# Feed-forward products in rows, 512 wide, with transposed hidden tiles, in a transformer kernel on one core

## The chip, the core and the metric

One core of a Trainium2 chip runs the whole program. Its engines work side by side and hand over by semaphores: TensorE (PE in the profile; PEld is its load of the stationary operand), VectorE (DVE), ScalarE (ACT), GpSimd (POOL) and SyncE (SP, which issues the loads here). Each engine carries out its own instructions in the order in which they are written. SBUF is the working memory of 128 partitions, PSUM (`ps`, 8 banks of 128 x 512 float32) takes TensorE's results. The metric is the device time of one execution in microseconds (us); lower is better.

## The reference

256 tokens of width 1024, float32, go through two blocks, one stage after the other. Each stage is `x = x + rms_norm(f(rms_norm(x, g_pre)), g_post)`, in the second block's feed-forward stages with a factor of 0.5 on the added part. The nine stages are:

```
moba    spatial gating, block attention of 8 heads and a causal convolution, then w_out
cross   attention to 256 rows of memory, 4 heads of 256
relu    square(relu(h @ w_ff1)) @ w_ff2, hidden width 4096
glu0    (silu(h @ wg) * (h @ wu)) @ wd, hidden width 2816
diff    differential attention, 8 heads of 2 x 64, rotary
glu1    as glu0
glu2    as glu0 (second layer)
near    neighborhood attention, 16 heads of 64
glu3    as glu0
```

`rms_norm(x, g)` is `x * rsqrt(mean(x * x) + 1e-6) * g` by token.

## The kernel before

**Products.** Float32 accuracy comes from splitting each operand into a high part of type float32r and the rest (low part), and adding three products: high x high, low x high, high x low. Weights come in chunks of 1 MB (`CH` = 2048 columns of 128 partitions): SP loads a chunk into one of three `raw` slots, ScalarE casts it to `w_hi` (L504, in loops L513), VectorE subtracts to `w_lo` (L756, in loops L765), TensorE uses it and signals `used`. 226 chunks are used, in one fixed order. Chunk c + 3 is split when chunk c has been used.

**Two forms of product.** `transposed_product` (L1146 to L1148) keeps a 128 x 128 block of weights in the array and streams the 256 tokens of `hT`: 48 matmuls of 256 columns a chunk; the result has features in partitions. `rows_product` (L1160 to L1162) keeps 128 tokens in the array and streams weights: the result has tokens in partitions. Down and output products are such, 24 matmuls of 512 columns a chunk, into the four banks `ps[2t + nb]` for token half t and column half nb. Values (`v`, `w`, `V`) are rows too, 256 columns wide.

**Feed-forward stages.** They run in loops (`Fori`) over blocks of 256 hidden columns: a gate chunk (bank 4), an up chunk (bank 5) and a down chunk; relu has only up and down. ScalarE applies Silu or Relu (`gate`), VectorE multiplies (`hraw`), and as the result already has features in partitions, it is cast and split to `hid_hi` and `hid_lo` (L683, L1053) and is the stationary operand of the down product.

**Attention stages.** `PLAN` writes out the order of the words for every engine: `q0` is a chunk, `rot0` a rotary step, a number an attention step, `o0` an output chunk. In step s the scores of unit s are computed, the probabilities of unit s - 1 are transposed (L1207) and the values of unit s - 2 weighed; in diff the result of unit s - 3 is transposed too. Products of chunks stand between the steps and fill TensorE while VectorE and ScalarE work on the softmax.

**The norm between two stages.** For token half t: ScalarE squares the two banks of y and sums (L541), POOL takes the root (L445, L446), VectorE multiplies y by the gain (L805) and adds it to x (L815), then multiplies x by the next gain into `t1` (L780). ScalarE squares x (L524), POOL takes the next root, VectorE writes it on a diagonal (L789), and TensorE multiplies `t1` by the diagonal in 8 matmuls, which transposes and scales at once (`turn`, L1175). ScalarE casts the two banks to `hT_hi` (L531), VectorE subtracts to `hT_lo` (L795). VectorE's order is written out: scale_y(0), add_y(0), gain_rows(0), scale_y(1), diagonal(0), add_y(1), gain_rows(1), low part 0, diagonal(1), low parts 1 to 3, and after them two splits of chunks. ScalarE: four squares of y, four of x, four casts, one split. The next stage's first product waits for `h_lo` of both halves.

## Time and profile before

| | |
|---|---|
| three runs, us | 1544.32, 1548.31, 1548.76 (median 1548.31) |
| profiled execution, us | 1547.44, of which span of the trace 1545.7 |
| mean granted TensorE clock | 0.981 |
| instructions | 24401 |
| PE busy | 1462.8 us, 95% |
| DVE busy | 856.8 us, 55% |
| ACT busy | 681.0 us, 44% |
| POOL busy | 141.8 us, 9% |
| loads | 255.95 MB, mean 166 GB/s |

Busy time is what an engine spends in instructions; a busy PE is not one at its peak, since matmuls overlap, so the distance between the starts of two matmuls says more than the duration of one. The granted clock is the share of 2.4 GHz that TensorE was given; it has two levels, 1.2 and 2.4 GHz. The time of an execution is the span and some 1.7 us around it.

### The profile page before, as it was taken

What the parts mean: (1) busy time and instruction counts of PE and PEld (TensorE: products, weight loads), DVE (VectorE), ACT (ScalarE), POOL (GpSimd) and SP (SyncE); (2) the same over time, 40 slices, a digit from 0 to 9 for tenths busy, and PEclk for the clock granted to TensorE, in tenths of its full rate; (3) what the DMA queues carried; (4) which work ended last, traced back from release to release, by engine and by line L of the source; (5) the groups of instructions that cost most, each with busy time, mean ns of one, the idle gap of its engine ahead of it and who ended that gap; (6) DMA issues with size and microseconds to landing.
All of it is one profiled execution on the core that took longest, in us unless ns stands there. A gap on an engine that the chain in (4) does not pass through costs nothing.

```text
span 1545.7 us, 24401 instructions
## 1 busy us (share of the span) xinstructions
PE 1462.8 (95%) x9945; PEld 1341.6 (87%) x9945; DVE 856.8 (55%) x912; ACT 681.0 (44%) x878; POOL 141.8 (9%) x248
## 2 busy tenths in 40 slices
PE   6999898999989999898889999899998999899996
PEld 6997687999989999897779999899997887799996
DVE  4976546555565454567655444655445656554443
ACT  5455444444453334445444433434434544444432
POOL 1000101111010110100111110111102300100000
PEclk9999999999999999999999999999999999999998
DMA  9654243565645566342336556465654534265551
GB/s 291 197 187 137 86 160 114 192 195 194 213 128 190 193 196 217 123 153 91 128 111 196 194 181 214 131 198 194 195 189 141 164 109 137 63 210 190 183 179 59
DMA packets 186889, 255.95 MB, mean 166 GB/s; under 512 B 6280, under 2 KB 163660, under 8 KB 186828
## 3 DMA queue, kind: packets, MB, share of 16 engines
q1 hardware_dynamic: 182732, 251.94, 50.0%
q0 software_dynamic: 4096, 3.15, 0.7%
q8 instruction: 43, 0.70, 0.2%
q14 instruction: 18, 0.15, 0.0%
HBM read 254.02 MB, written 1.05 MB: 165 GB/s over the span
## 4 chain that ended last, share of the span: by engine, by line
PE 89%; DVE 3%; ACT 3%; POOL 2%; issue 1%; DMA 1%; SPq 0%; DVEq 0%; POOLq 0%; ACTq 0%
PE ps L1146 17%; PE ps L1147 17%; PE ps L1148 17%; PE ps L1160 11%; PE ps L1161 10%; PE ps L1162 10%; PE ps L1175 2%; PE ps L1235 2%; PE ps L1196 2%; PE ps L1207 1%; DVE w_lo L756 1%; POOL rstd L445 1%; POOL rstd L446 1%; ACT t L565 1%; DMA raw<-w_in 1%
## 5 line engine op out<-in xcount | busy, mean ns | idle before, releaser
L1146 PE MATMUL ps<-hT_hi,w_hi 128*128 128x256 f32 x2096 | 597.7, 285 | 6.2 <-DVE hT_lo L795 4.8
L1147 PE MATMUL ps<-hT_lo,w_hi 128*128 128x256 f32 x2096 | 593.5, 283 | 0.0
L1148 PE MATMUL ps<-hT_hi,w_lo 128*128 128x256 f32 x2096 | 593.4, 283 | 0.0
L765 DVE TENSOR_TENSOR w_lo<-raw,w_hi 128x2048 fp32r<-128x2048 f32 x132 | 302.6, 2292 | 231.4 <-ACT w_hi L513 231.4
L1146 PEld LDWEIGHTS ps<-hT_hi,w_hi 128*128 128x128 f32 x2096 | 402.6, 192 | 12.5 <-issue 8.5
L1147 PEld LDWEIGHTS ps<-hT_lo,w_hi 128*128 128x128 f32 x2096 | 402.6, 192 | 2.6 <-issue 0.5
L1148 PEld LDWEIGHTS ps<-hT_hi,w_lo 128*128 128x128 f32 x2096 | 402.5, 192 | 0.0
L513 ACT CAST w_hi<-raw 128x2048 fp32r<-128x2048 f32 x132 | 250.9, 1901 | 118.6 <-PE ps L1148 118.6
L756 DVE TENSOR_TENSOR w_lo<-raw,w_hi 128x2048 fp32r<-128x2048 f32 x94 | 215.8, 2303 | 83.8 <-ACT w_hi L504 83.5
L504 ACT CAST w_hi<-raw 128x2048 fp32r<-128x2048 f32 x94 | 179.0, 1904 | 52.3 <-PE ps L1148 24.0
L1160 PE MATMUL ps<-w_hi,hid_hi 128*128 128x512 f32 x440 | 171.9, 391 | 0.0
L1161 PE MATMUL ps<-w_lo,hid_hi 128*128 128x512 f32 x440 | 171.8, 391 | 0.0
L1162 PE MATMUL ps<-w_hi,hid_lo 128*128 128x512 f32 x440 | 171.2, 389 | 0.0
L433 POOL DMA_DIRECT2D big<-na_rpb x128 | 66.1, 517 | 565.4 <-PE ps L1148 384.6
L683 ACT CAST hid_hi<-t 128x512 fp32r<-128x512 f32 x55 | 34.1, 620 | 174.2 <-PE ps L1162 174.2
L1175 PE MATMUL ps<-rope_t,t 128*128 128x128 f32 x320 | 58.9, 361 | 46.4 <-DVE rope_t L789 46.4
L1175 PEld LDWEIGHTS ps<-rope_t,t 128*128 128x128 f32 x320 | 55.2, 269 | 51.4 <-issue 51.4
L1162 PEld LDWEIGHTS ps<-w_hi,hid_lo 128*128 128x128 f32 x440 | 82.6, 188 | 17.6
L1160 PEld LDWEIGHTS ps<-w_hi,hid_hi 128*128 128x128 f32 x440 | 82.8, 188 | 15.7
L1161 PEld LDWEIGHTS ps<-w_lo,hid_hi 128*128 128x128 f32 x440 | 82.8, 188 | 15.1
L1160 PE MATMUL ps<-w_hi,yT_hi 128*128 128x512 f32 (+1 forms) x232 | 86.0, 371 | 3.1 <-DVE yT_lo L1014 3.0
L1053 DVE TENSOR_TENSOR hid_lo<-t,hid_hi 128x512 fp32r<-128x512 f32 x55 | 38.1, 692 | 90.6 <-ACT hid_hi L683 90.6
(162 smaller groups left out, 1506.9 us busy)
## 6 DMA issues: line engine op xcount, KB each, us to landing
raw<-ffn_wg SPq DMA_DIRECT2D x44, 1024.0 KB, 5.6
raw<-ffn_wu SPq DMA_DIRECT2D x44, 1024.0 KB, 5.6
raw<-ffn_wd SPq DMA_DIRECT2D x44, 1024.0 KB, 5.2
raw<-w_ff SPq DMA_DIRECT2D x32, 1024.0 KB, 5.4
raw<-diff_w_in SPq DMA_DIRECT2D x12, 1024.0 KB, 5.1
raw<-na_w_in SPq DMA_DIRECT2D x12, 1024.0 KB, 5.1
raw<-w_in SPq DMA_DIRECT2D x10, 1024.0 KB, 5.7
raw<-w_xkv SPq DMA_DIRECT2D x8, 1024.0 KB, 5.5
```

The source lines that it names most:

```text
L433: pool.dma_start(bias[p:p + 1], bass.AP(rpb.tensor, (5 - r) * 31 + 15 - c, [[465, 16], [31, 6], [1, 64]])).then_inc(bias_in, 16)
L504: act.copy(w_hi[:, slot, :], raw[:, slot, :]).then_inc(hi_done, 1)
L513: act.copy(w_hi[:, slot, :], raw[:, slot, :]).then_inc(hi_done, 1)
L756: dve.tensor_tensor(w_lo[:, slot, :], raw[:, slot, :], w_hi[:, slot, :], ALU.subtract).then_inc(lo_done, 1)
L765: dve.tensor_tensor(w_lo[:, slot, :], raw[:, slot, :], w_hi[:, slot, :], ALU.subtract).then_inc(lo_done, 1)
L1146: pe.matmul(o, hi, src[0][:, k, :], start=(k == 0), stop=False)
L1147: pe.matmul(o, hi, src[1][:, k, :], start=False, stop=False)
L1148: ins = pe.matmul(o, lo, src[0][:, k, :], start=False, stop=(k == KT - 1))
L1160: pe.matmul(o, hi, wh[:, i, cols], start=first and i == 0, stop=False)
L1161: pe.matmul(o, hi, wl[:, i, cols], start=False, stop=False)
L1162: ins = pe.matmul(o, lo, wh[:, i, cols], start=False, stop=last and i == len(tiles) - 1)
L1175: ins = pe.matmul(ps[:, 4 + 2 * t + b, k * P:(k + 1) * P], t1[:, t, col:col + P], diag[:, t, :], start=True, stop=True)
```

## The change

The feed-forward stages no longer use the transposed form for gate and up. They are now rows products over blocks of 512 hidden columns: chunk `ga` holds the first four tiles of 128 input features by 512 columns, `gb` the other four, and both add into one bank a token half (`up`). ScalarE's Silu or Relu and VectorE's multiplication give `hraw` with tokens in partitions; TensorE transposes it back in 128 x 128 blocks (`hidden_turn`, word `T`) into the bank of the up product, and the cast and the low part go from there to `yT`, which is the stationary operand of the down product. The last block of a gated stage is 256 wide (`g`, `u`, `d`). The values of diff and near are computed so too, ahead of q and k (`va` to `vd`), into banks 4 to 7.

Where the next stage is a feed-forward stage (`LATE_SCALE`), the pre-norm's root isn't put on a diagonal: `turn` is a plain transpose, and `rstd` is the scale of Silu or Relu and of the multiplication (in relu it enters twice, in a gated stage once in each factor).

There are four slots for split weights in these stages; the fourth lies over `qT` and `kT` (`w_hi_3`, `w_lo_3`). `raw` keeps three. All loops are gone: the whole program is a list of words in `PLAN`, which all engines read. `s` is a split of the next chunk on ScalarE and VectorE, `h` on ScalarE alone, `l` on VectorE alone; `q1.0` and `q1.1` are the halves of a product. `G` and `H` are activation and multiplication of a block, `T` its transposing with cast and low part.

The norm is five words for each token half: `post` (squares of y, root, scale, add), `gain`, `sq` (squares of x, root, and the diagonal where there is one), `turn` (transposing, casts, low parts), with 0 at the end of a stage and 1 at the head of the next. Each engine carries out its part of each word in the order of the words. The gains are loaded at the seventh and eighth chunk of a stage.

Core of the diff:

```diff
+HEAD_GLU = "post1 s gain1 s turn1 sq1 ga0 s gb0 G0.0 G0.1 s ua0 s ub0 H0.0 H0.1 s "
+BLOCK_GLU = ("ga{b} s T{a} gb{b} G{b}.0 G{b}.1 s ua{b} s ub{b} H{b}.0 H{b}.1 s da{a} s db{a} s ")
+LAST_GLU = ("g5 T4 G5.0 G5.1 s u5 H5.0 H5.1 s da4 T5 ")
+GLU = HEAD_GLU + "".join(BLOCK_GLU.format(a=b - 1, b=b) for b in range(1, 5)) + LAST_GLU
+HEAD_RELU = ("post1 s gain1 s turn1 sq1 ua0 s ub0 G0.0 H0.0 G0.1 H0.1 s ua1 s T0 "
+             "ub1 G1.0 H1.0 G1.1 H1.1 s da0 s db0 s ")
+BLOCK_RELU = "ua{b} s T{a} ub{b} G{b}.0 H{b}.0 G{b}.1 H{b}.1 s da{a} s db{a} s "
+RELU = (HEAD_RELU + "".join(BLOCK_RELU.format(a=b - 1, b=b) for b in range(2, 7)) +
+        "ua7 s T6 ub7 G7.0 H7.0 G7.1 H7.1 s da6 T7 s db6 s da7 db7 ")
+HEAD_V = "post1 s gain1 sq1 s turn1 va0 s vb0 s vc0 "
+PLAN = {
...
+    "relu": RELU + "post0 gain0 turn0 sq0",
+    "glu0": GLU + "s db4 d5 post0 gain0 sq0 turn0",
...
+    "diff": (HEAD_V + "s vd0 "
+             "q0 s k0 s rot0 q1.0 rot4 q1.1 h lambda 0 l k1.0 rot1 k1.1 h 1 l q2.0 rot5 q2.1 h 2 l "
+             "k2.0 rot2 k2.1 h 3 l q3.0 rot6 q3.1 h 4 l k3.0 rot3 k3.1 h 5 l rot7 o0.0 6 o0.1 h 7 l "
+             "o1.0 8 o1.1 s 9 s o2 10 o3 post0 gain0 turn0 sq0"),
+    "glu1": GLU + "s db4 d5 post0 gain0 turn0 sq0",
+    "glu2": GLU + "s db4 d5 post0 gain0 sq0 turn0",
+    "near": (HEAD_V + "vd0 s "
...
+             "q0 s k0 s 0 q1.0 1 q1.1 h 2 l k1.0 3 k1.1 h 4 l q2.0 5 q2.1 h 6 l k2.0 7 k2.1 h 8 l "
...
+    "glu3": GLU + "db4 d5 post0 end1",
...
+LATE_SCALE = {i + 1 for i, kind in enumerate(STAGES) if kind in FFN}
...
+    held, slots, before = [-1] * 4, [], []
+    for c, (kind, name, _) in enumerate(CHUNKS):
+        free = range(4) if kind in FFN or name in ("va", "vb", "vc", "vd") else range(3)
+        slot = min(free, key=lambda s: held[s])
+        slots.append(slot)
+        before.append(held[slot])
+        held[slot] = c
...
+        w_hi_3 = nc.alloc_sbuf_tensor_at("w_hi_3", [P, CH], F32R, offset=qk_end - 16 * KT * P)
+        w_lo_3 = nc.alloc_sbuf_tensor_at("w_lo_3", [P, CH], F32R, offset=qk_end - 8 * KT * P)
...
-        hraw = t1[:, 0, 0:512]
-        gate = t1[:, 0, 512:1024]
...
+        def turn_bank(n, t, b):
+            return ps[:, 5 + 2 * b if n >= 2 else 4 + 2 * t + b, :]
+        def up_bank(kind, b, t):
+            return ps[:, (4 + 2 * (b % 2) if kind == "relu" else 6) + t, :]
...
+                if c == FIRST[at] + 6:
+                    load_post_gain(at)
+                load(c, src, dims)
+                if c == FIRST[at] + 7 and at < N_NORMS - 1:
+                    load_pre_gain(2 + at)
...
+            def norm_word(word):
+                t, j, n = norm_at(word)
+                if word.name in ("post", "end"):
                     for b in range(2):
+                        if b == 0:
+                            act.wait_ge(y_bank, 2 * j + t + 1)
                         else:
+                            act.wait_ge((half_used, used)[t], LAST[j] + 1)
+                        count = 2 * (TT * j + t) + b + 1
+                        square(ps[:, 2 * t + b, :], b, ssq[:, 32 + TT * j + t, b:b + 1], sq_post, count)
+                if word.name == "sq":
+                    for b in range(2):
+                        act.wait_ge(x_new, 2 * (TT * j + t) + b + 1)
+                        count = 2 * (TT * n + t) + b + 1
+                        square(x[:, t, 512 * b:512 * b + 512], b, ssq[:, TT * n + t, b:b + 1], sq_pre, count)
...
+                    src = up_bank(kind, b, t) if kind == "relu" else ps[:, 4 + t, :]
+                    act.activation(gate[:, t, 0:width], src[:, 0:width], ACT.Relu if kind == "relu" else ACT.Silu,
+                                   scale=rstd[:, k:k + 1]).then_inc(gate_done, 1)
...
+            def norm_word(word):
+                t, j, n = norm_at(word)
+                if word.name in ("post", "end"):
+                    scale_y(j, t)
+                    add_y(j, t)
+                if word.name == "gain":
+                    gain_rows(n, x, t)
+                if word.name == "sq" and n not in LATE_SCALE:
+                    diagonal(n, t)
+                if word.name == "turn":
+                    turned_lo(n, t, hT)
...
+            def hidden_word(kind, word):
+                b, t, beta = word.digit, word.half, B0[kind] + word.digit
+                if word.name == "H":
+                    last = "b" if kind == "relu" or b < 5 else ""
+                    width = 256 if kind != "relu" and b == 5 else 512
+                    dve.wait_ge((half_used, used)[t], AT_CHUNK[kind, "u" + last, b] + 1)
+                    dve.wait_ge(gate_done, TT * beta + t + 1)
+                    if b:
+                        dve.wait_ge(hid_turned, TT * (beta - 1) + t + 1)
+                    k = TT * (word.at + 1) + t
+                    dve.scalar_tensor_tensor(hraw[:, t, 0:width], up_bank(kind, b, t)[:, 0:width], rstd[:, k:k + 1],
+                                             gate[:, t, 0:width], ALU.mult, ALU.mult).then_inc(hraw_done, 1)
...
+            def turn(n, t):
+                if n >= 2 and t:
+                    pe.wait_ge(h_lo, 4 * n + 2)
+                late = n in LATE_SCALE
+                if not late:
+                    pe.wait_ge(diag_set, len([m for m in range(n) if m not in LATE_SCALE]) * TT + t + 1)
+                for b in range(2):
+                    pe.wait_ge(normed, 2 * (TT * n + t) + b + 1)
+                    for k in range(4):
+                        rows, to = t1[:, t, P * (4 * b + k):P * (4 * b + k) + P], turn_bank(n, t, b)[:, k * P:(k + 1) * P]
+                        if late:
+                            ins = pe.transpose(to, rows, ident)
+                        else:
+                            ins = pe.matmul(to, rows, diag[:, t, :], start=True, stop=True)
+                    ins.then_inc(turned, 1)
...
+            def hidden_turn(kind, word):
+                b, beta = word.digit, B0[kind] + word.digit
+                for t in range(TT):
+                    pe.wait_ge(hraw_done, TT * beta + t + 1)
+                    for i in range(len(hid_tiles(kind, b))):
+                        cols = slice(i * P, i * P + P)
+                        ins = pe.transpose(up_bank(kind, b, t)[:, cols], hraw[:, t, cols], ident)
+                    ins.then_inc(hid_turned, 1)
...
+            def up(kind, word):
+                b, beta = word.digit, B0[kind] + word.digit
+                short = len(word.name) == 1
+                first, last = word.name[1:] in ("a", ""), word.name[1:] in ("b", "")
+                tiles = range(KT) if short else range(4 * last, 4 * last + 4)
+                width = 256 if short else 512
+                for t in halves_of(word):
+                    for i in range(2) if short else (int(last),):
+                        h_ready(word.at + 1, t, i)
+                    if first and kind == "relu" and b >= 2:
+                        pe.wait_ge(hid_lo, TT * (beta - 2) + t + 1)
+                    if first and kind != "relu" and b >= 1:
+                        if word.name[0] == "g":
+                            pe.wait_ge(gate_done, TT * (beta - 1) + t + 1)
+                        else:
+                            pe.wait_ge(hid_lo, TT * (beta - 1) + t + 1)
+                    o = ps[:, 4 + t, :] if word.name[0] == "g" else up_bank(kind, b, t)
+                    finish(in_rows(hT, tiles, word, width, o[:, 0:width], t, 0, first, last), word, t)
...
+            def values(kind, word):
+                i = "abcd".index(word.name[1])
+                for t in halves_of(word):
+                    h_ready(word.at + 1, t, i % 2)
+                    o = ps[:, 4 + 2 * (i // 2) + t, :]
+                    tiles = range(4 * (i % 2), 4 * (i % 2) + 4)
+                    finish(in_rows(hT, tiles, word, 512, o, t, 0, i % 2 == 0, i % 2 == 1), word, t)
```

In `turn`, n >= 2 and t = 1 waits for the low parts of half 0, since both halves now use banks 5 and 7. Words in which an engine has no part are skipped by it; TensorE has none in `post`, `gain` and `sq`.

## Rows read from the trace of the kernel before

**Rows 1.** The page, busy us (share of the span) x instructions.

```profile
PE 1462.8 (95%) x9945; PEld 1341.6 (87%) x9945; DVE 856.8 (55%) x912; ACT 681.0 (44%) x878; POOL 141.8 (9%) x248
```

**Rows 2.** Busy us by stretch, last product of a stage to next product.

```profile
core 0: us, PE busy (x) PEld busy (x) DVE busy (x) ACT busy (x) POOL busy (x), PEclk, DMA share, GB/s
439.10:450.36 11.26, 6.73 (x33) 6.19 (x33) 8.14 (x14) 5.61 (x15) 3.46 (x6) 0.70 0.00 0
...
1184.06:1196.07 12.01, 6.39 (x33) 5.94 (x33) 8.87 (x14) 4.94 (x13) 8.18 (x11) 0.72 0.00 0
...
175.17:185.62 10.45, 5.70 (x33) 5.24 (x33) 8.15 (x14) 5.61 (x15) 3.46 (x6) 0.84 0.00 0
...
sum 88.53, PE 50.04 PEld 46.15 DVE 66.19 ACT 42.77 POOL 32.42; mean PE 6.25 PEld 5.77 DVE 8.27 ACT 5.35 POOL 4.05
```

**Rows 3.** The same view: relu, glu0, diff and near, first to last product.

```profile
257.54:439.10 181.56, 180.11 (x1152) 164.05 (x1152) 97.97 (x69) 79.04 (x71) 17.48 (x34) 1.00 0.60 195
450.36:637.19 186.83, 186.83 (x1320) 176.12 (x1320) 93.30 (x60) 77.12 (x63) 17.34 (x34) 1.00 0.60 195
648.40:788.28 139.88, 125.53 (x880) 114.10 (x880) 88.07 (x139) 66.50 (x149) 10.44 (x18) 0.98 0.39 128
1196.07:1334.68 138.61, 136.92 (x866) 112.42 (x864) 80.95 (x141) 67.30 (x124) 17.77 (x14) 1.00 0.40 130
```

**Rows 4.** Timeline, PE: start us, us, line, op, out<-in, shape; two product forms.

```profile
245.04 0.39 PE L1160 MATMUL ps<-w_hi,yT_hi 128*128 128x512 f32 x1
...
246.18 0.39 PE L1162 MATMUL ps<-w_hi,yT_lo 128*128 128x512 f32 x1
...
460.02 0.28 PE L1148 MATMUL ps<-hT_hi,w_lo 128*128 128x256 f32 x1
...
460.74 0.28 PE L1148 MATMUL ps<-hT_hi,w_lo 128*128 128x256 f32 x1
```

**Rows 5.** Timeline, PE: four transposes of probabilities and the next product.

```profile
120.18 0.66 PE L1207 MATMUL ps<-tab,prob 128*128 128x128 f32 x4
120.59 0.36 PE L1146 MATMUL ps<-hT_hi,w_hi 128*128 128x256 f32 x1
```

**Rows 6.** Timeline, relu to glu0: ACT, DVE and POOL; in brackets idle before.

```profile
437.37 0.30 POOL L445 TENSOR_SCALAR rstd<-ssq 128x1 f32<-128x1 f32 x1 [25.50 <-ACT probT L541]
...
438.34 1.42 DVE L815 SCALAR_TENSOR_TENSOR x_rows<-t,rstd,x_rows 128x512 f32<-128x512 f32 x2 [0.35 <-POOL rstd L446]
...
439.30 0.60 ACT L541 ACTIVATE prob<-ps 128x512 f32<-128x512 f32 x1 [0.67 <-PE ps L1162]
...
439.68 1.28 DVE L780 TENSOR_TENSOR t<-x_rows,gain 128x512 f32<-128x512 f32 x2
...
448.91 0.59 ACT L531 CAST hT_hi<-ps 128x512 fp32r<-128x512 f32 x1 [1.34 <-PE ps L1175]
...
450.28 1.92 ACT L504 CAST w_hi<-raw 128x2048 fp32r<-128x2048 f32 x1
...
450.42 0.69 DVE L795 TENSOR_TENSOR hT_lo<-ps,hT_hi 128x512 fp32r<-128x512 f32 x1 [0.20 <-ACT hT_hi L531]
451.03 2.28 DVE L756 TENSOR_TENSOR w_lo<-raw,w_hi 128x2048 fp32r<-128x2048 f32 x1
```

**Rows 7.** Timeline, PE: the last product of relu.

```profile
438.87 0.39 PE L1162 MATMUL ps<-w_hi,yT_lo 128*128 128x512 f32 x1
```

**Rows 8.** Busy us by stretch, columns as in rows 2: the low clock.

```profile
443.19:448.63 5.44, 5.44 (x24) 5.19 (x25) 3.96 (x7) 2.56 (x6) 1.08 (x2) 0.50 0.00 0
...
178.98:182.39 3.41, 3.12 (x15) 3.15 (x15) 3.09 (x6) 1.97 (x5) 1.01 (x2) 0.50 0.00 0
```

**Rows 9.** Timeline, DVE: two low parts in diff, one step in near.

```profile
733.55 0.42 DVE L1014 TENSOR_TENSOR yT_lo<-ps,yT_hi 128x256 fp32r<-128x256 f32 x1
...
744.58 0.42 DVE L1014 TENSOR_TENSOR yT_lo<-ps,yT_hi 128x256 fp32r<-128x256 f32 x1
...
1244.29 0.76 DVE L954 SCALAR_TENSOR_TENSOR att_bias<-ps,big 128x256 f32<-128x256 f32 x2 [1.66 <-PE ps L1196]
```

**Rows 10.** Timeline, PE: weighing the values in one step of diff.

```profile
734.12 1.13 PE L1222 MATMUL ps<-vv,probT 128*128 128x128 f32 x8 [1.42 <-DVE yT_lo L1014]
```

904 lines of the change are left out of this document (386 added, 518 removed), and 14 rows, old and new, of the table PLAN.

## The prediction

> **What bounds the kernel now.** I read the busy table first: TensorE is busy for 95% of the span [rows 1], so only what changes its own work or its pauses can matter. Then the table by stretches [rows 2, 3], cut at every point where TensorE starts no product for over 10 us. Eight such stretches, the norms between two stages, sum to 88.53 us [rows 2]. They are 10.45 us (moba to cross; cross to relu the same), 12.01 us (glu2 to near) and between 10.5 and 11.3 us for the rest. Between them TensorE is full: in glu0 186.83 us busy of 186.83 [rows 3], in relu 180.11 of 181.56, in near 136.92 of 138.61. Only diff has real pauses, 14 of 139.88 us. Third, the distance of matmul starts: 256-wide products start every 0.12 us (460.02 to 460.74, six steps), 512-wide ones every 0.228 us (245.04 to 246.18, five steps) [rows 4]. A chunk of weights is 48 narrow or 24 wide matmuls, 5.76 or 5.46 us; glu0's 22 up and gate chunks and 11 down chunks give 22 x 5.76 + 11 x 5.46 = 186.8, the measured length. So the model of products is right, and the loops of that stage cost nothing that can be seen. Last, the timeline of one norm, relu to glu0 [rows 6, 7]. I call E the end of the last product there: last start 438.87 + 0.23 = 439.10. The next product starts 11.26 us later [rows 2].
>
> **Wide products.** These narrow chunks become wide: 16 in relu, 20 of 22 in each gated stage (the last gate and up chunk stay 256 wide), 4 values chunks each in diff and near. Each saves 5.76 - 5.46 = 0.30 us: relu -4.8, each gated stage -6.0, diff and near -1.2 each; together -31.2.
>
> **The transposes this buys.** A hidden block of 512 in rows needs 8 transposes before the down product: 8 blocks in relu, five of 8 and one of 4 in each gated stage, 240 in all. The same operation stands in the attention steps: four transposes start at 120.18 and the next product follows at 120.59 [rows 5]. That is 0.41 us for four, plus about 0.1 for leaving a product: 1.0 for eight, 0.6 for four. Relu +8.0, each gated stage +5.6, together +30.4. Bounds: 0.82 us a group of eight (nothing lost at the ends) to 1.2. The Trainium skill (TensorE: Matmul & The Clock Gate, Part 4: PE-mode transpose) gives about 275 ns for one such transpose in a kernel; 240 of them would then be 66 us and the total 40 us higher. The row of this case has starts 0.11 us apart and decides.
>
> Does TensorE wait for these hidden tiles? A T word is written one to three chunks behind the product that makes its rows, 5.5 us or more, while activation and multiply take 0.6 + 0.7. After T, ScalarE first casts a chunk (1.92), then two tiles (0.59 each), VectorE splits (2.28), then takes the low parts (0.69): about 5.0 us to the first half [rows 6]. The next user (ua after gb) comes 1.0 + 5.46 = 6.5 us after T began, so 1.5 us are spare. The exception is T4 then u5 in the gated stages: u5 writes the bank that T4 fills. First four transposes 0.7, cast 0.6, low part 0.7 and hand-overs: 2.1 against 1.0 of TensorE work, a stall of 1.1 us, four times: +4.4.
>
> Against measured stages: a gated stage becomes 31 x 5.46 + 2 x 5.76 + 5.6 + 1.1 = 187.5 for 186.83 (+0.6, four times +2.4); relu 32 x 5.46 + 8.0 = 182.7 for 181.56 (+1.2; that stage also loses a wait of its own). **Feed-forward stages: +3.6.**
>
> **The row scale.** Moving the scale from the diagonal to gate and up costs nothing: same instructions with a scalar operand. It takes the root and the diagonal off the chain of the norm. **Four weight slots, no loops.** Splits ran one chunk ahead already without TensorE waiting; nothing is gained, and nothing lost, since hand-written stretches like near run as densely as looped ones [rows 3]. **Queue of SP.** The gains are loaded at the stage's seventh and eighth chunk; their waits (y_scaled and normed of the norm before) are long met, and 0.5 MB beside chunks that come three buffers ahead is hidden. **Queue of POOL.** The roots stand in the order of the words and the 128 loads of na_rpb keep their counts of used chunks, none ahead of a root that a product waits for: nothing.
>
> **The norm between stages.** This decides. In after, both VectorE and ScalarE execute it word by word: post0 gain0 turn0 sq0 | post1 s gain1 s turn1 sq1. Token half 1 can start only when half 0 has gone through TensorE and back, and two chunk splits stand inside it; TensorE stands at turn1, which is written before ga0. With durations of [rows 6, 7], in us after E: add of half 0 ends 0.66 and its gain 1.86 (both as before); turn0's second four transposes give their bank at 2.7; two casts 3.3; ScalarE then squares x (a pair, 2 x 0.6 + 0.1 = 1.3) to 4.6, and only then y of half 1, whose bank was ready at 0.2, to 6.0; POOL's root with its hand-overs (437.37 to the add's start at 438.34), 7.0; add 1.42, 8.45; the split s 2.28, 10.75 (its ScalarE cast is over at 7.9); gain 1.28, 12.05; turn1's last four transposes at half clock, twice the 0.41, 12.95. There ga0's half 0 starts: it needs nothing of half 1, whose low parts come (behind the second split) at 15.0, before its 12 matmuls are over. So 12.95 instead of 11.3 (or 10.5) us. Five stages begin so: cross to relu, relu to glu0, diff to glu1, glu1 to glu2, near to glu3.
>
> The three into attention (sq0 before turn0) keep the diagonal: x squared 1.5, root 2.5, diagonal 2.85, turn0 4.2, casts 4.9, y squared 6.2, root 7.2, add 8.6, split 10.9, gain 12.2, diagonal 12.5, eight slow turns 14.5. diff and near start va0 there: 14.5. cross starts with q0, which needs both halves: cast 0.59 and low parts 0.69 more, 15.95. Sum: 5 x 12.95 + 2 x 14.5 + 15.95 = 109.7 against 88.53: **+21.2**. Bounds: if each hand-over is 0.1 us shorter or POOL's root 0.6 us longer, as it is elsewhere, -8 to +8.
>
> **The clock.** Before, it is at its lower level (1.2 GHz) for a part of each norm: the granted share over a norm is 0.70 to 0.84 [rows 2]. TensorE takes up work inside the low part and has 3.12 us (178.98 to 182.39) or 5.44 us (443.19 to 448.63) of it behind it when the clock is back [rows 8]. The 16 turns absorb that, so products start at 2.4 GHz. After, TensorE does 1 us of turn0, pauses until E + 11.45, and products follow the few transposes at once. With 4.3 us to come back the clock rises at E + 15.8: 2.8 us of products at half speed, 1.4 lost, five times 7.0; diff and near 1.2 each, cross 0.5. **+10**, bounds 0 (risen by the transposes) and 18 (the longer return everywhere).
>
> **diff and near.** The values chunks go ahead of the attention steps, which are then filled by halves of q, k and output chunks. near: two half-chunk steps take 11.4 us of TensorE; VectorE has 1.66 us idle in such a pair already [rows 9], so it stays TensorE's: -1.2 + 0.6 for the first step's chain = -0.6. diff: six steps carry a rope and a split; VectorE needs 11.0 us for one (low part at 733.55 to low part at 744.58) and holds TensorE up by 1.42 us [rows 9, 10]. Those keep their length; the steps with half chunks and no rope come down to 7 to 9 us from 8 to 10 us; the front gets 40.4 instead of 31.5 us. Sum 139 for 139.88: -1, with -6 and +5 as bounds, for I had to lay these steps in a row from single durations. moba and cross keep their order.
>
> **Sum.** +3.6 + 21.2 + 10 - 1 - 0.6 = +33.2 on the profiled execution's 1547.44 us (span 1545.7): 1580.6. The median of the three runs is 0.9 us higher. I take 1581.
>
> **Rivals.**
> (a) The norm is set by the data alone, not by the written order: the squares of y of half 1 follow its bank, and the splits fall elsewhere. Then E + 0.2, squares 1.5, root 2.5, add 3.9, gain 5.2, turn 5.6: 5.6 us for late-scale stages, 7.5 for diff and near, 9 for cross, 52 in all instead of 88.5, hardly any slow clock: -36.5 + 3.6 - 1.6, about **1513**. For it: the chain with no root and diagonal is really shorter, and half 0 alone opens the stage. Against it: each engine takes its queue in order, and VectorE is in between for at least one split. It decides if half 1's add ends before E + 5 rather than at 8.5.
> (b) The gaps stay as they are (the shorter chain and the splits just cancel) and the clock is up in time: only +3.6 - 1.6: **1549**, no change.
> (c) Hidden tiles come late in every block, as the spare 1.5 us is used up by cast or split order: 1 us each in 30 blocks, **1611**. Against: those engines are half idle in glu0 (93 and 77 of 187 us).
> (d) Turns of late-scale stages leave the clock low for their 1.4 us too, half of it lost five times: 3.5 more, **1584**. The Trainium skill (the same section) says that transposes don't count as busy for the clock; no row here has them alone with a low clock, while the turns of [rows 8] are true matmuls.
>
> **Chances.** Forecast 0.66 (own range 1560 to 1600: norms, clock and diff near their ends), (d) 0.05, (c) 0.09, (b) 0.06, (a) 0.14. The range leaves out (a) and the far end of (c): 1546 to 1611. About 0.3%, 4.6 us, is what a measurement of this kernel tells from none. Faster than that 0.14, within 0.06, slower 0.80.
>
> **What would show it.** Right: stretches without product of 13 to 16 us, with squares of y (t=1) some 4.7 us after E, a split between the second add and the second gain; slow clock over the first matmuls of a stage; glu0 187 to 190 us from first to last product; transposes 0.11 us apart. Wrong: stretches under 10 us, waits of ua on hidden tiles, or values chunks in diff leaving the steps idle by over 15 us more.

## The result, and the profile of the changed kernel

The changed kernel takes 1614.03 us (median of 4 runs, 1613.15 to 1616.0); the kernel before took 1547.92 us in 4 runs beside it (1544.32 to 1548.76). The ratio is 1.0434, with a 95% interval from 1.0414 to 1.0453. So it is slower, as forecast, but by 66 us and not by 33, and just outside the range.

The profiled execution took 1616.0 us, its span is 1614.3 us, the mean granted clock 0.955 for 0.981. From the page, the busy line (as rows 1):

```profile
PE 1460.8 (90%) x7609; PEld 1236.1 (77%) x7609; DVE 852.2 (53%) x910; ACT 688.8 (43%) x886; POOL 142.0 (9%) x248
```

TensorE has 2336 instructions fewer and is busy for 2 us less, but its share fell from 95% to 90%: the added time is pauses, and products at the low clock.

The stretches from the last product of a stage to the next product, columns as in rows 2:

```profile
180.00:200.12 20.12, 7.24 (x33) 6.54 (x33) 11.20 (x16) 8.08 (x17) 4.81 (x6) 0.67 0.22 79
...
458.89:471.51 12.62, 3.01 (x17) 2.46 (x17) 10.39 (x13) 7.62 (x13) 1.72 (x4) 0.68 0.08 16
659.10:677.87 18.77, 7.35 (x34) 6.93 (x33) 12.72 (x16) 9.29 (x17) 4.82 (x6) 0.56 0.23 79
...
1238.84:1258.12 19.28, 7.14 (x33) 6.82 (x33) 14.06 (x16) 9.28 (x17) 9.37 (x9) 0.66 0.25 82
...
sum 121.30, PE 36.77 PEld 32.59 DVE 90.00 ACT 64.74 POOL 27.62; mean PE 4.09 PEld 3.62 DVE 10.00 ACT 7.19 POOL 3.07
```

These are moba to cross, relu to glu0, glu0 to diff, glu2 to near. The five norms ahead of a feed-forward stage are alike (12.61 to 12.65 us). All eight sum to 121.3 for 88.53 us [rows 2]: **+32.8**. (The means in the last row count a ninth stretch, of 0.01 us.)

The same view of the stages relu, glu0, diff and near, first to last product:

```profile
275.91:458.89 182.98, 182.98 (x834) 151.80 (x832) 94.14 (x69) 78.59 (x72) 18.39 (x36) 0.99 0.59 193
471.51:659.10 187.59, 186.53 (x886) 156.44 (x884) 90.26 (x62) 76.40 (x66) 18.25 (x36) 0.99 0.59 194
677.87:837.96 160.09, 131.04 (x786) 113.73 (x785) 84.20 (x137) 63.41 (x145) 10.44 (x18) 0.90 0.32 103
...
1258.12:1401.62 143.50, 137.30 (x770) 108.67 (x769) 75.61 (x140) 63.15 (x120) 17.98 (x16) 0.99 0.34 114
```

Against rows 3: relu +1.4, glu0 +0.8, **diff +20.2**, near +4.9. In diff TensorE pauses for 29.1 us where it paused for 14.4 (+14.7), and is busy for 131.04 us for 125.53 (+5.5) at a mean clock of 0.90 for 0.98. The other stages, from the same starts and ends of products: moba +4.8 (0.4 of it ahead of its first product), cross +1.7, all five feed-forward stages together +4.1. Nothing is added behind the last product. This is 68.6 us, by which the two profiled executions differ too.

Where the low clock falls differs from kernel to kernel, and this moves stages that an edit doesn't touch. cross takes 61.46 us (within 0.01) in the kernel before and in every run that has no low clock in it, and 63.18 here, where 3.9 us of it are at the low clock:

```profile
200.12:263.30 63.18, 62.50 (x368) 56.41 (x368) 26.98 (x35) 24.54 (x39) 0.86 (x2) 0.97 0.37 125
```

moba, ahead of every norm, takes 161.1 us with 3.4 us at the low clock in this kernel, and 163.4 with 10.2 in those of experiments 5 and 7. So a difference of one to three us between two kernels is put down to an edit below only where a row shows it.

### The profile page after: what moved, and what is told of

Same layout as the page of the kernel before. It is cut to its first block, busy times and chain, and to the rows that moved or that the text cites. A ratio compares the mean times of both kernels' runs of the same rounds, so it can differ in the third digit from the quotient of the medians.

```text
span 1614.3 us, 18455 instructions
## 1 busy us (share of the span) xinstructions
PE 1460.8 (90%) x7609; PEld 1236.1 (77%) x7609; DVE 852.2 (53%) x910; ACT 688.8 (43%) x886; POOL 142.0 (9%) x248
## 3 DMA queue, kind: packets, MB, share of 16 engines
HBM read 254.02 MB, written 1.05 MB: 158 GB/s over the span
## 4 chain that ended last, share of the span: by engine, by line
PE 85%; DVE 5%; ACT 4%; issue 3%; POOL 2%; DMA 1%; SPq 0%; DVEq 0%; ACTq 0%; POOLq 0%
PE ps L1107 22%; PE ps L1109 22%; PE ps L1108 22%; PE ps L1093 4%; PE ps L1094 3%; PE ps L1095 3%; PE ps L1184 2%; PE ps L1145 2%; PE ps L1126 2%; PE ps L1333 2%; DVE w_lo L771 1%; ACT probT L560 1%; PE ps L1156 1%; DVE x_rows L820 1%; POOL rstd L487 1%
## 5 line engine op out<-in xcount | busy, mean ns | idle before, releaser
L1107 PE MATMUL ps<-w_hi,hT_hi 128*128 128x512 f32 (+1 forms) x1008 | 380.3, 377 | 4.2 <-DVE yT_lo L1060 4.2
L1108 PE MATMUL ps<-w_lo,hT_hi 128*128 128x512 f32 (+1 forms) x1008 | 375.6, 373 | 0.0
L1109 PE MATMUL ps<-w_hi,hT_lo 128*128 128x512 f32 (+1 forms) x1008 | 375.5, 373 | 0.0
L1107 PE MATMUL ps<-w_hi,yT_hi 128*128 128x512 f32 (+1 forms) x672 | 260.2, 387 | 13.3 <-DVE rope_t L1035 7.5
L1109 PE MATMUL ps<-w_hi,yT_lo 128*128 128x512 f32 (+1 forms) x672 | 257.1, 383 | 0.0
L1107 PEld LDWEIGHTS ps<-w_hi,hT_hi 128*128 128x128 f32 x1008 | 192.0, 190 | 37.4 <-issue 5.5
L1109 PEld LDWEIGHTS ps<-w_hi,hT_lo 128*128 128x128 f32 x1008 | 191.3, 190 | 33.5
L1107 PEld LDWEIGHTS ps<-w_hi,yT_hi 128*128 128x128 f32 x672 | 127.8, 190 | 42.4 <-DVE w_lo L771 12.1
L1093 PE MATMUL ps<-hT_hi,w_hi 128*128 128x256 f32 x432 | 128.5, 298 | 3.2 <-DVE hT_lo L800 3.2
L1094 PE MATMUL ps<-hT_lo,w_hi 128*128 128x256 f32 x432 | 123.7, 286 | 0.0
L1095 PE MATMUL ps<-hT_hi,w_lo 128*128 128x256 f32 x432 | 123.4, 286 | 0.0
L1093 PEld LDWEIGHTS ps<-hT_hi,w_hi 128*128 128x128 f32 x432 | 84.4, 195 | 9.3 <-issue 8.9
L1094 PEld LDWEIGHTS ps<-hT_lo,w_hi 128*128 128x128 f32 x432 | 84.4, 195 | 0.8 <-issue 0.5
L1095 PEld LDWEIGHTS ps<-hT_hi,w_lo 128*128 128x128 f32 x432 | 84.3, 195 | 0.0
```

What stands on the lines that cost most here:

```text
L1093: pe.matmul(o, hi, src[0][:, k, tokens], start=(k == 0), stop=False)
L1094: pe.matmul(o, hi, src[1][:, k, tokens], start=False, stop=False)
L1095: ins = pe.matmul(o, lo, src[0][:, k, tokens], start=False, stop=(k == KT - 1))
L1107: pe.matmul(o, hi, wh[:, i, cols], start=first and i == 0, stop=False)
L1108: pe.matmul(o, hi, wl[:, i, cols], start=False, stop=False)
L1109: ins = pe.matmul(o, lo, wh[:, i, cols], start=False, stop=last and i == len(tiles) - 1)
```

## Where each part of the time comes from

**A norm ahead of a feed-forward stage.** Timeline of relu to glu0 (start, duration, engine, line, operation; in brackets idle before), as rows 6; E, the last product's end, is 458.89:

```profile
465.56 1.41 DVE L820 SCALAR_TENSOR_TENSOR x_rows<-t,rstd,x_rows 128x512 f32<-128x512 f32 x2 [0.33 <-POOL rstd L487]
466.89 2.28 DVE L771 TENSOR_TENSOR w_lo<-raw,w_hi 128x2048 fp32r<-128x2048 f32 x1
469.09 1.28 DVE L785 TENSOR_TENSOR t<-x_rows,gain 128x512 f32<-128x512 f32 x2
469.92 1.94 PE L1124 MATMUL ps<-tab,t 128*128 128x128 f32 x8 [8.45 <-DVE t L785]
...
471.51 0.78 PE L1107 MATMUL ps<-w_hi,hT_hi 128*128 128x512 f32 x1
```

This is the forecast order: squares of y after squares of x, the add, a split between add and gain, the turn, the product at E + 12.62. TensorE idles for 8.45 us until half 1's gain is there.

**A norm ahead of attention.** Same view, glu0 to diff, E = 659.10:

```profile
662.15 3.79 PE L1126 MATMUL ps<-rope_t,t 128*128 128x128 f32 x16 [2.89 <-DVE rope_t L794]
...
670.13 2.29 DVE L771 TENSOR_TENSOR w_lo<-raw,w_hi 128x2048 fp32r<-128x2048 f32 x1
...
671.07 2.03 POOL L486 TENSOR_SCALAR rstd<-ssq 128x1 f32<-128x1 f32 x1 [2.31 <-ACT probT L560]
...
673.19 0.85 POOL L487 TENSOR_TENSOR rstd<-rstd,minus_half 128x1 f32<-128x1 f32 x1
674.08 0.29 DVE L794 TENSOR_SCALAR rope_t<-tab,rstd 128x128 f32<-128x128 f32 x1 [0.45 <-POOL rstd L487]
...
674.46 3.75 PE L1126 MATMUL ps<-rope_t,t 128*128 128x128 f32 x16 [8.53 <-DVE rope_t L794]
```

The eight matmuls with the diagonal are recorded as **x16**, two instructions ("passes" below) each: a turn is 3.8 us at the low clock, while the eight plain transposes of the fence above take 1.9, at the low clock too. I had priced both kinds by the count of instructions. And the root of half 1 waits on POOL: its two instructions take 2.03 and 0.85 us beside VectorE's split of a chunk, for 0.30 [rows 6] and some 0.56 us elsewhere. The first takes 2.03 us in all three norms ahead of attention, where it runs beside a split, and 0.52 in the same place of experiment 1, where the split is gone and only a gain runs beside it:

```profile
665.36 0.52 POOL L486 TENSOR_SCALAR rstd<-ssq 128x1 f32<-128x1 f32 x1 [2.30 <-ACT probT L560]
```

**diff.** TensorE waited over the whole kernel (us in total, times, longest), the first row of these for the norm's diagonals:

```profile
PE ps L1126 <- DVE rope_t L794: 45.7, 7, 10.8
PE ps L1107 <- DVE rope_t L1035: 7.5, 1, 7.5
PE ps L1145 <- issue: 5.8, 1, 5.8
...
PE ps L1107 <- DVE yT_lo L1060: 4.2, 4, 1.1
```

The places behind the third and the second of these rows, in TensorE's and VectorE's timeline:

```profile
738.40 2.29 DVE L771 TENSOR_TENSOR w_lo<-raw,w_hi 128x2048 fp32r<-128x2048 f32 x1
...
741.92 0.69 DVE L1039 TENSOR_TENSOR kT<-kT,rope_t 128x512 f32<-128x512 f32 x1
742.72 2.08 PE L1145 MATMUL ps<-kT,qT 64*128 64x256 f32 x8 [5.83 <-issue]
...
789.53 2.28 DVE L771 TENSOR_TENSOR w_lo<-raw,w_hi 128x2048 fp32r<-128x2048 f32 x1
791.73 0.68 DVE L1035 TENSOR_TENSOR rope_t<-ps,tab 128x512 f32<-128x512 f32 x1
...
792.66 0.77 PE L1107 MATMUL ps<-w_hi,yT_hi 128*128 128x512 f32 x1 [7.47 <-DVE rope_t L1035]
```

The first pause is put down to "issue", but the scores at 742.72 need `kT`, which VectorE ends at 742.6: the rotary step stands in the plan half a chunk before the attention step that uses it, and VectorE does a chunk's split first. A pause of 2.6 us ahead of 767.8 is the same. The third, 7.5 us, is the first output product, which waits for `rope_mul` 8 because it writes the banks of the last rotary step, again behind a split. In diff, waits for rotary steps are thus 17.4 us (7.5, 5.8 and two of 4.1 together), where the kernel before had 1.7. Of the others, the one for `yT_lo` fell from 9.4 to 5.4 us and the one for `sub_out` rose from 1.6 to 5.2.

**The end of moba.** The plan now splits a chunk ahead of the last attention step. In moba:

```profile
168.14 1.90 ACT L554 CAST w_hi<-raw 128x2048 fp32r<-128x2048 f32 x1 [3.42 <-PE ps L1109]
...
170.07 2.29 DVE L771 TENSOR_TENSOR w_lo<-raw,w_hi 128x2048 fp32r<-128x2048 f32 x1 [4.78 <-ACT w_hi L554]
172.28 0.42 DVE L1009 TENSOR_TENSOR yT_lo<-ps,yT_hi 128x256 fp32r<-128x256 f32 x1
...
172.84 0.47 PE L1107 MATMUL ps<-w_hi,yT_hi 128*128 128x512 f32 x1 [3.79 <-DVE yT_lo L1009]
```

Both halves of the split stand ahead of the two small operations that the last output product needs, and TensorE waits for 3.8 us, where it waited for 1.0 before. In near the same wait is 1.0 us, as before.

**near.** TensorE's waits between its first and last product:

```profile
PE ps L1145 <- ACT kT L698: 2.8, 4, 0.8
PE ps L1156 <- DVE prob L974: 2.4, 1, 2.4
```

The kernel before had the first once (0.7 us) and the second not at all. The 2.4 us are in the second attention step: the transposes of the first probabilities wait for the softmax, and only half a chunk stands in between.

## Experiments

Each kernel is the changed kernel with the edit shown, unless it says otherwise. Times are medians of 4 runs, the ratio is to the kernel before on the same chip (medians 1547.49, 1548.44, 1548.22 and 1549.78 us). The changed kernel is named C: 1614.03 us.

### 1. Chunk splits behind the norm

```diff
-HEAD_GLU = "post1 s gain1 s turn1 sq1 ga0
+HEAD_GLU = "post1 gain1 turn1 sq1 s s ga0
-HEAD_V = "post1 s gain1 sq1 s turn1 va0
+HEAD_V = "post1 gain1 sq1 turn1 s s va0
```

relu and cross are altered likewise.

> The changed kernel with the chunk splits of each stage's head moved behind turn1 (before they stood between post1 and gain1, and between gain1 and turn1). Theory W (the written order of the words sets the norm): in every norm one split of 2.3 us on VectorE leaves the chain, so the stretch without product falls from 12.6 to 10.3 us before a feed-forward stage and from 18.8 to 20.1 to some 16 to 17 us before an attention stage: 8 x 2.3 = 18 us less, 1596 us; a little more if POOL's root, slowed to 2.9 us beside a split, runs in 0.9. Rival C (the low clock is what costs, the split only fills a wait that another step sets): the stretches keep their length within 0.5 us, 1612 us.

Measured: 1603.77 us (ratio 1.036, 1.0342 to 1.0377), between the two expectations. Each feed-forward norm is 10.41 us for 12.62, so the split inside the norm costs 2.2 us, as its duration says; the attention norms lose 1.8 to 2.9. All norms together are 17.6 us shorter in the profile, but the stages are 4.3 us longer: glu3 takes 188.66 for 187.32 us,

```profile
1399.74:1588.40 188.66, 187.60 (x886) 157.20 (x884) 89.27 (x61) 76.78 (x68) 1.72 (x4) 0.99 0.47 159
```

with 4.4 us of its products at the low clock for 1.5. With the norm shorter, more of the low stretch lies on products. Of the 4.3 us, 2.6 are in feed-forward stages and 1.1 in near, which this explains; 1.1 are in moba, ahead of all norms. About a fifth of the gain is given back so.

### 2. Chunk splits behind the last attention step

```diff
-             "o1.0 8 o1.1 s 9 o2 post0 gain0 sq0 turn0"),
+             "o1.0 8 o1.1 9 s o2 post0 gain0 sq0 turn0"),
```

cross, diff and near likewise.

> The changed kernel with the splits that stand before the last attention steps of moba, cross, diff and near moved behind those steps (s 9 becomes 9 s, and the like). Theory W: the cast and the low part of the last heads wait behind a split of 1.9 + 2.3 us on ScalarE and VectorE, which is why moba ends 4.8 us later than before the change, near 4.9 and cross 1.7; moba gets 3.2 to 4.8 us back, near, cross and diff together 3 to 5: 1605 to 1608 us. Rival C (the half-speed clock after other pauses accounts for these stages): under 2 us, 1612 to 1614 us.

Measured: 1610.98 us (1.0402, 1.0385 to 1.042), 3 us of the 6 to 9 expected. moba fell from 161.11 to 158.13 us, and its wait of 3.8 us to 1.0; the rest over its length before, 1.5 us, goes with 3.4 us at the low clock. near stayed at 143.56 and diff at 159.98: there the place of this split was not the cause. cross fell from 63.18 to 61.46 us, its length before, but it does so in experiment 3 too, where its splits stand as in C; both runs have no low clock in it:

```profile
200.71:262.17 61.46, 60.78 (x368) 54.67 (x368) 26.96 (x35) 24.50 (x39) 0.86 (x2) 1.00 0.38 129
```

So the split did not lengthen cross; the low clock did.

### 3. Rotary steps one step earlier in diff

```diff
-"q0 s k0 s rot0 q1.0 rot4 q1.1 h lambda 0 l k1.0 rot1 k1.1 h 1 l q2.0 rot5 q2.1 h 2 l "
+"q0 s k0 s rot0 q1.0 rot4 q1.1 h lambda 0 rot1 l k1.0 k1.1 h 1 rot5 l q2.0 q2.1 h 2 rot2 l "
```

The other rotary steps move likewise, and the wait for `rope_mul` 8 goes from the first output product to where its second token half starts.

> The changed kernel with diff's rotary words moved to stand directly behind an attention step and ahead of the split that follows it, and with the first output product waiting for the rotary multiplications (banks 2 and 3) only at its second token half, which is the half that writes these banks. Theory R (three pauses of TensorE in diff, 5.8, 2.6 and 7.5 us, come from ropes that are written just ahead of their user): all 7.5 us and some 5 of the other 8.4 go, and part comes back as pauses elsewhere: diff from 160.1 to 145 to 150 us, kernel 1599 to 1604 us. Rival V (diff is bound by the softmax chain on VectorE and ScalarE, now that its values product stands ahead of it): diff stays above 155 us, kernel 1609 to 1614 us.

Measured: 1604.09 us (1.0366, 1.0349 to 1.0384), at the upper end of what was expected. diff, first to last product:

```profile
674.46:823.29 148.83, 128.68 (x786) 111.86 (x785) 83.75 (x137) 63.39 (x145) 10.45 (x18) 0.95 0.33 111
```

11.3 of the 20.2 us are gone: 8.9 of pauses and 2.4 of busy time; the clock of the stage is 0.95 for 0.90. The wait of 7.5 us is gone, the other waits for rotary steps are 6.9 us for 9.9 (one of 3.6 and three of 3.3 together), and the one for `yT_lo` is back from 5.4 to 7.0. TensorE still pauses for 20 us here where it paused for 14, and is busy for 3.2 us more than before; these two make the 9 us that are left.

### 4. Half 1 not behind half 0

```diff
-HEAD_GLU = "post1 s gain1 s turn1 sq1 ga0
+HEAD_GLU = "ga0
+LATE = "post0 gain0 post1 turn0 sq0 s gain1 s turn1 sq1"
+FULL = "post0 gain0 sq0 post1 turn0 s gain1 sq1 s turn1"
```

The plans end with LATE or FULL in place of `post0 gain0 ... turn0`, so ScalarE squares y of half 1 before it casts half 0.

> The changed kernel with all words of a norm at the end of the stage and post1 ahead of turn0, so that ScalarE and VectorE treat y of token half 1 without waiting for half 0's way through TensorE; the two splits keep their places around gain1. Theory W: before a feed-forward stage 12.6 becomes 10.1 us, before an attention stage 3 to 4 us less: 20 to 23 us less in all, 1591 to 1594 us. Rival C: as TensorE pauses as long, the clock falls as before and the first matmuls keep half speed, so that the gain is the same 20 us only if the return of the clock follows TensorE's work; if it comes at fixed times the gain is 10 to 15 us, 1599 to 1604 us.

Measured: 1601.68 us (1.0337, 1.0319 to 1.0354), above the first expectation and inside the rival's. Feed-forward norms 10.87 to 10.90 us, attention norms 18.05, 15.29 and 17.37, all eight together 16.2 us less. The stages are 3.7 us longer, but 2.1 of that are in moba, ahead of all norms, with 10.0 us at the low clock there for 3.4; feed-forward stages are 1.6 longer and near 1.0. So neither the written order nor the splits alone make the norm long, each is worth about as much, and each is partly given back by the clock.

### 5. The turn's waits filled with transposes

```diff
+                if n >= 2 and (t or not late):
+                    for _ in range(70 if t else 20):
+                        pe.transpose(ps[:, 4, 0:P], ident, ident)
```

> The changed kernel with 70 transposes of the identity, whose result nobody reads, written ahead of every turn1, and 20 ahead of each turn0 that waits for a diagonal. At full clock they take 0.11 us each, 7.7 and 2.2 us, which fits into TensorE's waits of 8.5 and 2.9 us. Theory K (the low clock costs beside the waits): if transposes hold the clock, the turns into attention run 32 passes at 0.11 instead of 0.21 us, 3.4 us less three times, and the first matmuls of all stages run at full speed, 1.0 to 1.6 us less eight times: 1614 - 20 = 1594 us. Rival N (transposes do not hold the clock): the 70 run at 0.21 us, 14.9 us, and lengthen each norm by 4 to 6 us: 1650 to 1660 us. Rival W (the clock costs nothing, only waits do): 1612 to 1616 us.

### 6. The same with matmuls

```diff
+                    for _ in range(35 if t else 10):
+                        pe.matmul(ps[:, 4, 0:P], ident, ident, start=True, stop=True)
```

> As the run with transposes, but with 35 and 10 float32 matmuls of the identity instead (two passes of 0.11 us each, so the same TensorE time). Theory K: they hold the clock, 1594 us as with transposes. If only these and not the transposes hold it, this run gives 1594 and the other 1650 us or more. Rival W: 1612 to 1616 us.

Measured: 1602.43 us with transposes (1.0349, 1.0328 to 1.0371) and 1606.87 with matmuls (1.0371, 1.0346 to 1.0396), whose intervals overlap. Both are 8 us or more above the 1594 of the theory and below the 1612 of rival W. Of the run with transposes, relu to glu0, glu0, and glu0 to diff by stretch, and TensorE's timeline in the two norms:

```profile
456.97:469.43 12.46, 9.91 (x88) 9.33 (x87) 10.25 (x13) 7.30 (x13) 1.72 (x4) 1.00 0.09 15
469.43:656.00 186.57, 185.51 (x887) 155.82 (x886) 90.37 (x62) 76.42 (x66) 18.17 (x36) 1.00 0.59 195
656.00:671.90 15.90, 13.80 (x123) 13.37 (x122) 12.03 (x15) 9.29 (x17) 4.82 (x6) 1.00 0.20 66
```

```profile
460.94 7.86 PE L1119 MATMUL ps<-tab 128*128 128x128 f32 x70 [1.40 <-DVE hT_lo L800]
...
659.05 2.05 PE L1129 MATMUL ps<-rope_t,t 128*128 128x128 f32 x16 [0.70 <-DVE rope_t L794]
```

In these two norms 70 transposes that compute nothing hold the clock at 2.4 GHz, as 35 two-pass matmuls do, and the turn of 16 passes takes 2.05 us where it took 3.79. Five of the eight norms are so. In the other three (cross to relu, diff to glu1, near to glu3) the clock fell in the pause ahead of the 70, and came back while TensorE did nothing but these transposes. Cross to relu, from the first of the 70 to the return of the clock, and from there to the last:

```profile
265.58:268.51 2.93, 2.93 (x14) 2.93 (x15) 1.54 (x3) 2.93 (x7) 1.72 (x4) 0.50 0.00 0
268.51:274.69 6.18, 6.18 (x59) 6.18 (x58) 6.18 (x6) 2.27 (x2) 0.00 (x0) 1.00 0.26 68
```

In the whole trace 54.5 us are at the low clock for 145.9 in C. Rival (d) of the prediction is gone with that. The Trainium skill (TensorE: Matmul & The Clock Gate, Part 4: PE-mode transpose) says that full clock doesn't engage for transposes; by this trace it is held through 7.86 us of nothing else and comes back with nothing else, and the measurement decides.

The kernel is 11.6 us faster by the medians and 13.3 by the profiled executions, but the low clock's price is larger. These became shorter: feed-forward stages 5.7, diff 3.5, near 1.5, cross 1.7, the three attention norms 8.6, together 21.0. Others became longer. The five norms ahead of feed-forward stages took 5.1 more, as the filling itself was on the path where the clock had fallen: from diff to glu1 its 70 took 10.80 us for 7.86, and the norm 15.42 for 12.65. moba and the time ahead of its first product took 2.6 more, with 10.2 us at the low clock for 3.4. So the 11.6 us are what the filling was worth, and not what the clock cost.

### 7. Every hidden tile transposed twice

```diff
-                    for i in range(len(hid_tiles(kind, b))):
+                    for i in 2 * tuple(range(len(hid_tiles(kind, b)))):
```

> The changed kernel with every hidden tile transposed twice into the same place. Theory T (the 240 transposes lie wholly on TensorE's path, 0.11 us each, and what they cost is what the wide products save): 26 us more, 1640 us; 1 to 2 more where u5 waits for T4. Rival H (they lie beside waits of TensorE and are partly hidden): under 15 us more.

Measured: 1635.92 us (1.0565, 1.0544 to 1.0586), +21.9 on C for 26 expected. relu by stretch:

```profile
276.04:465.73 189.69, 189.69 (x898) 158.61 (x896) 94.20 (x69) 78.52 (x72) 18.33 (x36) 0.99 0.57 186
```

relu grew by 6.7 us for 64 more transposes, the five feed-forward stages together by 25.5 for 240: 0.106 us each, all of it on the path. The gap to the total is where the low clock fell: near came out at 141.97 us with none of it, for 143.51 with 4.1, cross at 61.45 for 63.18, and diff and the norms were 4.1 us shorter together, while moba took 2.3 more with 10.2 us of it for 3.4.

### 8. T4 ahead of g5

```diff
-LAST_GLU = ("g5 T4 G5.0 G5.1 s u5
+LAST_GLU = ("T4 g5 G5.0 G5.1 s u5
```

> The changed kernel with T4 ahead of g5 and nothing else: 4.2 us less, 1610 us, if the waits of u5 for T4's low parts are the whole of that stall. If g5's tiles or the activations take its place, under 1.5 us.

Measured: 1605.63 us (1.0371, 1.0347 to 1.0396), 8.4 less than C. The stall of `u5` on `T4` (the row L1107 <- yT_lo L1060 above, 1.05 us four times) is gone: the gated stages are 186.27, 185.84, 187.20 and 185.97 us. That is 5.2 us, 4.2 of which are the stall, as expected. The rest of the 8.4 lies in cross, in diff and in the norms ahead of attention, whose words are the same, and the whole trace has 134.4 us at the low clock for 145.9: it goes with the clock, and whether `T4`'s place moved that is not shown.

### 9. All reorderings of the plan at once

Experiments 2 and 3, and the norm without a split in it, with post1 and gain1 ahead of what they don't depend on:

```diff
+LATE = "post0 gain0 post1 turn0 gain1 turn1 sq0 sq1"
+FULL = "post0 gain0 sq0 post1 turn0 gain1 sq1 turn1"
-HEAD_GLU = "post1 s gain1 s turn1 sq1 ga0
+HEAD_GLU = "s s ga0
```

> The changed kernel with the ropes a step early and the splits behind the last steps, as in the single runs, and both changes of the norm together: post1 ahead of turn0 and no split inside the norm. Theory W: the norm in front of a feed-forward stage falls to 8 us, in front of an attention stage to 12.5 to 14 us; that is 4.6 x 5 + 5.5 x 3 = 39 us less waiting. The single runs gave back 1.0 to 1.5 us a stage to the slow clock, so 8 to 12 us return; with 3 and 10 us of the two other changes: 1614 - 39 + 10 - 13 = 1572 us. Rival P (the single gains do not add, as each shortens the same wait): 1588 us or more.

Measured: 1563.25 us (1.0092, 1.0071 to 1.0114), 9 us better than expected. Relu to glu0 by stretch, and VectorE in it:

```profile
446.16:454.08 7.92, 3.01 (x18) 2.46 (x17) 6.78 (x11) 2.33 (x5) 1.53 (x2) 0.82 0.00 0
```

```profile
449.14 1.40 DVE L822 SCALAR_TENSOR_TENSOR x_rows<-t,rstd,x_rows 128x512 f32<-128x512 f32 x2
450.46 1.28 DVE L802 TENSOR_TENSOR hT_lo<-ps,hT_hi 128x512 fp32r<-128x512 f32 x2
451.66 1.28 DVE L787 TENSOR_TENSOR t<-x_rows,gain 128x512 f32<-128x512 f32 x2
```

VectorE now has no pause until the last gain ends at 452.9, and nothing but the norm's own work is in its queue: 7.92 us, where the kernel before took 11.26 [rows 2]. All norms together take 82.4 us, 6 less than before the change: the five ahead of feed-forward stages, with the late row scale, 15.2 less, and the three ahead of attention, with the diagonal, 9.1 more. So the plan's order hid what the late row scale can give. How much of the 15.2 us is that scale is not shown, for the first product behind these norms also waits for half 0 alone. What else keeps the kernel 1% behind is in the stages: diff +9.5, feed-forward stages together +6.1, near +6.0, cross +1.6 on the kernel before.

### 10. Product halves around the norm

Experiment 9, with the first products of each stage and the last ones of the feed-forward stages cut into token halves, so that half 1's last product covers half 0's norm and half 0's first product covers half 1's. LATE and FULL have `turn0` ahead of `post1` again, and `turn1` stands in the head of the next stage:

```diff
-HEAD_GLU = "s s ga0 s gb0 G0.0
+HEAD_GLU = "ga0.0 gb0.0 sq1 turn1 s s ga0.1 s gb0.1 G0.0
-    "glu1": GLU + "s db4 d5 " + LATE,
+    "glu1": GLU + "s db4.0 d5.0 db4.1 d5.1 " + LATE,
-    "cross": ("s q0 s q1 h 0
+    "cross": ("q0:0 q1:0 turn1 s q0:1 s q1:1 h 0
```

> The changed kernel with the ropes and last splits of the single runs, and with token halves of products written over the norm: the last two chunks of a feed-forward stage go first for half 0 and then for half 1, and the first two chunks of every next stage do half 0 ahead of turn1; splits stand behind turn1. Theory W: TensorE then waits some 1.3 us for the low parts of half 0 and 0.8 us for those of half 1, in place of one wait of 7 to 12 us, and has no pause long enough for the clock to fall: against e8, 3 to 4 us less in each of eight norms, 1 us of slow products less in each: 1563 - 28 - 8 = 1527 us. Rival Q (ScalarE and VectorE, which still carry out half 1 behind half 0, now set the norm): half 1 comes 3 to 4 us later than that, 1545 to 1555 us.

### 11. The same, and T4 ahead of g5

> As e9, with the word T4 ahead of the chunk g5 in the gated stages, so that u5 no longer follows the transposes whose bank it writes: 1.05 us less in each of four stages, 4 us less than e9.

Measured: 1557.77 us (1.0063, 1.0039 to 1.0087) and 1550.36 us in 10 runs (1.0016, 1.0001 to 1.0031). The second minus the first is -7.4, near the -8.4 of experiment 8. But the first missed its expectation of 1527 by 31 us, although a norm ahead of a feed-forward stage now costs TensorE two or three pauses of about 1 us. In the second kernel, moba to the third chunk of cross, then the first of the two runs of query products in it, cut where the clock falls, then the second run (it falls there too, at 210.71):

```profile
177.37:231.42 54.05, 48.17 (x232) 47.29 (x233) 13.43 (x17) 12.72 (x21) 3.02 (x6) 0.59 0.18 65
...
185.29:186.81 1.52, 1.52 (x14) 1.52 (x14) 1.19 (x3) 0.30 (x2) 0.86 (x2) 1.00 0.00 0
186.81:204.61 17.80, 17.80 (x86) 17.80 (x85) 2.76 (x5) 1.39 (x4) 1.08 (x2) 0.50 0.01 1
...
209.28:228.70 19.42, 19.42 (x97) 19.42 (x98) 4.58 (x2) 3.32 (x3) 0.00 (x0) 0.54 0.40 136
```

Here a half is the transposed form: 128 columns an instruction instead of 256, 96 of them twice. TensorE is busy without a pause in both runs. Both begin at the upper level, fall to the lower one 1.5 us later in the middle of the work, and stay there for 20.5 us, past their end: 38.7 us for work that took 13.4 in experiment 9.

Two things add up in this. The first is the number of instructions. Starts are 0.112 us apart at the upper level with 128 columns and 0.12 with 256, so 192 halves instead of 96 whole ones would cost some 21.5 us for 11.5 at the upper level alone. The second is the clock: at the lower level starts are 0.213 us apart, and this is the other 17 us.

### 12. Whole query products in cross

Experiment 11 with one line changed:

```diff
-    "cross": ("q0:0 q1:0 turn1 s q0:1 s q1:1 h 0
+    "cross": ("turn1 s q0 s q1 h 0
```

> Edit: the kernel with product halves over the norm and with T4 ahead of g5, with one line of the plan changed: cross begins with turn1 and the whole products q0 and q1 (256 tokens wide), not with their halves of 128 tokens around turn1. Nothing is left out. In the run before it those halves ran from 185.29 to 204.61 and from 209.28 to 228.70, 96 instructions each, at a granted clock of 0.56: 0.20 us for an instruction that moves 128 columns, and 54.1 us from the last product of moba (177.37) to the first one behind the two query chunks (231.42). In the kernel that turned both halves together ahead of the whole products the same distance was 175.97 to 206.40, 30.4 us, of which the 96 products took 13.4. Theory (the narrow products keep the clock low, and are what the missing gain of the last two kernels went to): this distance falls from 54.1 to about 30.5, the two low stretches of 20.5 us become one of about 13, and the kernel runs in about 1527, ahead of the kernel before. Rival (the low clock belongs to the turn and its two pauses, whatever the product behind it): the low stretch stays over 20 us long with wide products too, the distance falls by the lost pauses alone, under 10 us, and the time is 1541 or more. Second rival: the turn in two with its pauses back (3.8 and 1.5 us) costs what the whole products save: no change, 1550.

Measured: **1527.74 us** (1525.54 to 1530.31), beside 1549.78 for the kernel before; ratio **0.9859** (0.9837 to 0.988). It is faster than both kernels, than the one before by 1.4%. The same distance, and the low stretch:

```profile
175.94:209.41 33.47, 22.38 (x137) 21.67 (x137) 13.44 (x17) 11.67 (x21) 3.01 (x6) 0.69 0.22 81
...
177.90:198.50 20.60, 11.47 (x50) 10.94 (x51) 9.45 (x13) 6.69 (x13) 2.48 (x5) 0.50 0.00 2
```

The distance fell by 20.6 us, with the 96 query products down to 13.5, with three pauses (2.9, 6.7, 1.5 us) inside it. One low stretch of 20.5 us is left of two, longer than the 13 expected, but all except 4 us of it lie on pauses and the turn; the distance is 33.5 us for 30.5 expected. Both rivals had the time at 1541 or above and fall. The low clock on these products comes with the halves, and not with the turn ahead of them: with halves the clock was up when they started and fell under them, and with whole products behind the same kind of turn it was down when they started and came back 4 us later. The edited line also has one run of products and one stretch of pauses in place of two, so it doesn't part the price of the clock from that of the doubled instructions; the distances between starts above do.

Against the kernel before, each feed-forward stage with the norm ahead of it is now shorter (relu 2.6, glu0 8.6, glu1 7.1, glu2 7.7, glu3 7.4 us); cross with its norm is 10.1 us longer and diff 3.6; moba and near are level.

## Why the prediction was half right

**Right.** The direction, and the main reason: words executed in their written order put half 1's norm behind half 0 and behind a split. The feed-forward norm was forecast at 12.95 and is 12.62 us, each step in its place; rival (a) gave 5.6 for the data alone, and with the order changed experiment 9 comes as far as 7.92. The stall of u5 on T4 was forecast at 1.1 us and is 1.05, four times (the waits of C; gone in experiment 8). The wide products: at full clock (experiment 5) glu0 is 186.57 us, and 31 x 5.46 + 2 x 5.76 = 180.8 leaves 5.8 for 44 transposes and that stall, so 0.108 us a transpose. The feed-forward stages were forecast at +3.6 without the clock's share; at full clock they are at -1.5.

**The term of the transposes, slightly too high.** I took 1.0 us for a group of eight, with 0.82 as the lower bound. It is 0.85 (experiment 7: 0.106 each), so +25.5 and not +30.4. The other price that the prediction names, 66 us for the 240 (the page measured its transpose in bf16), is 36 us above its own term and not 40. Rival (c) did not happen: only the T4 stall shows among TensorE's waits on hidden tiles.

**The clock, about right on products, left out elsewhere.** Forecast +10 with 0 to 18, all of it on the products behind a norm. Experiment 5 takes 5.7 us from feed-forward stages (forecast 7.0), 3.5 from diff and 1.5 from near (1.2 each) and 1.7 from cross (0.5): 12.4 for 9.9, though diff's share belongs in part to pauses of its own. The attention norms, of which I had priced only the last turn as slow, hold 8.6 more.

**The norms ahead of attention, mis-sized.** Step "eight slow turns 14.5" and "turn0 4.2": forecast 14.5, 14.5 and 15.95, measured 18.8, 19.3 and 20.1, together +13.2 on the forecast. For glu0 to diff the surplus of 4.3 us splits so: turn0 ends at E + 6.8 and not 4.2 (+2.6, of which 2.3 are left when half 1's gain ends), and everything of half 1 follows it; POOL's slow root beside the split +0.4; turn1, from the diagonal to the first product, 3.5 instead of 2.0 (+1.5). The cause could have been read from the trace of before: I used the price of a transpose of probabilities for a matmul with a diagonal, although [rows 2] have 33 records of TensorE in a norm of 16 such matmuls. The bounds of -8 to +8 on the norms did not hold the surplus of 11.6 us (13.2 less 1.6 that the feed-forward norms came out shorter) either, since they stood on hand-overs and POOL alone.

**diff, the step that failed.** Forecast -1 with bounds of -6 and +5, measured +20.2: the largest error of all. I compared the sum of VectorE's work in a step with the sum of TensorE's, and never asked what stands directly ahead of its user. Three just-in-time places cost 5.8, 2.6 and 7.5 us; experiment 3 takes 11.3 of the stage's 20.2 away, and experiment 5 takes 3.5 by the clock (the two may overlap). The 9 us that experiment 3 leaves are 5.8 of pauses, where rotary steps still come late, and 3.2 of busy time; no run takes these apart further.

**moba, cross, near.** Forecast 0, 0 and -0.6, measured +4.8, +1.7 and +4.9. "moba and cross keep their order" was wrong for moba: its words for chunks and steps kept their order, but the split `s` moved ahead of the last attention step. Experiment 2 shows 3.0 us to be this; most of the rest goes with 3.4 us at the low clock. cross's +1.7 is the low clock behind its norm, forecast at 0.5. In near, 1.5 us are the clock (experiment 5) and the waits above are 4.5 more than before; with 1.2 saved by the wide products that is 4.8. The term "+0.6 for the first step's chain" was too small: that one wait is 2.4 us, and the four for `kT`, of which the kernel before had one, add 2.1.

**The sum.** On the forecast's +33.2: norms +11.6 (the clock inside them included), diff +21.2, near +5.5, moba +4.8, cross +1.7, and feed-forward stages with clock +4.1 instead of 3.6 + 7.0, which is -6.5. The clock's other share of the forecast, 3 us, was for diff, near and cross and is in their measured values: -3. This gives +68.5, the measured difference within its rounding.

## What to carry to other kernels

When an order is written out word by word, price it word by word: for each operation that TensorE waits for, list what stands ahead of it on its own engine, above all a long operation that nobody needs yet, such as the split of a chunk. Sums over a step or a stage say what could be reached, not what happens. Before you shorten a pause, look where the low clock will lie afterwards. Take the price of a matmul from the records of that same kind of matmul, their count included. And before you read a gain of a few us as the work of an edit, look at the stages that the edit does not touch.

## What the runs showed of the hardware

- A float32 matmul with a diagonal of 128 columns is recorded as two passes (x16 for eight instructions), 3.79 us at the low clock and 2.05 at the full one; a transpose of the same size is one pass, 1.94 us for eight at the low clock and 1.04 at the full one (C and experiment 5).
- Transposes held the granted clock at 1.00 through 7.86 us of nothing else, and it came back from 0.50 to 1.00 in 2.93 us of nothing else (experiment 5).
- Products with their own weights and 128 columns ran back to back for 19.3 us, twice; the clock was up when they started, fell 1.5 us later and stayed down to their end. In the same place, with 256 columns, it was down when they started and up 4 us later (experiments 11 and 12).
- With their own weights each, starts of products are 0.112 us apart with 128 columns, 0.12 with 256 and 0.228 with 512 at the full clock. At the low clock they are 0.213 us apart with 128 and with 256 columns alike (experiment 11; near in C, 1301.50 to 1302.78), and 0.43 with 512 (moba in C, 173.83 to 174.69).
- A POOL operation that reads 128 x 1 elements took 2.03 us beside a 2.29 us split on VectorE in three norms of three, 0.52 in the same place beside a gain (experiment 1), and 0.30 beside an idle VectorE.
